# Expert inputs of a two-layer hybrid transformer: rows gathered from DRAM, or made on chip as products with one-hot matrices

## What is computed

```python
def hier_moe(xt, w_rg, b_rg, w_re, b_re, w_g, w_u, w_d):
    lg = xt @ w_rg + b_rg                      # 4 groups
    gi = argmax(lg)                            # top-1 group
    top_v, top_i = top_k(le_of_group, 2)       # 8 experts in it, the best 2
    wts = pg_top * softmax(top_v)
    ...
    xd = zeros(...).at[dest].set(xt[t_s])      # token rows sorted by expert
    hid = silu(xb @ w_g[e]) * (xb @ w_u[e])    # for each expert e, 1024 -> 256
    yd = hid @ w_d[e]                          # 256 -> 1024
    return zeros(n, d).at[t_s].add(yd[dest] * w_s)
```

## Time and profile before

| | before |
|---|---|
| median of 3 runs | 1564.5 us (1563.03 to 1565.46) |
| the profiled execution: its time / span of its instructions | 1567.55 / 1565.7 us |
| PE busy | 1233.9 us, 79% |
| DVE busy | 598.4 us, 38% |
| ACT busy | 445.4 us, 28% |
| POOL busy | 154.1 us, 10% |
| moved by DMA | 388.11 MB, mean 248 GB/s |

### The profile page before, as it was taken

One profiled execution on the slowest core, in us unless ns is written; L12 is line 12 of the kernel. 1 busy time (PEld: TensorE's weight loads), 2 busy tenths in 40 slices (PEclk: granted clock), 3 DMA queues, 4 the chain that ended last, 5 costly groups with the idle time before them and its releaser, 6 DMA issues. The chain is left out here.

```text
span 1565.7 us, 20477 instructions
## 1 busy us (share of the span) xinstructions
PE 1233.9 (79%) x8036; PEld 892.6 (57%) x8036; DVE 598.4 (38%) x1223; ACT 445.4 (28%) x993; POOL 154.1 (10%) x147
## 2 busy tenths in 40 slices
PE   3799798999999648888777259988999478788871
PEld 1589665688879535444343149855999344344430
DVE  0534586354454531111110274575677511111102
ACT  1233266533343310000000244355665210001002
POOL 1601000011112210000000330000012200000002
PEclk9899999999999769899899769989999689889996
DMA  9994168623322138999999905358554179999993
GB/s 321 300 387 140 55 216 298 187 88 101 108 81 82 41 138 339 422 422 422 412 422 390 299 27 135 108 186 263 171 170 167 76 291 423 421 423 411 422 423 129
DMA packets 150543, 388.11 MB, mean 248 GB/s; under 512 B 35232, under 2 KB 96672, under 8 KB 125888
## 3 DMA queue, kind: packets, MB, share of 16 engines
q1 hardware_dynamic: 123424, 315.95, 54.5%
q10 hardware_dynamic: 18784, 41.61, 7.1%
q0 software_dynamic: 8256, 29.46, 4.8%
HBM read 346.09 MB, written 40.89 MB: 247 GB/s over the span
## 5 line engine op out<-in xcount | busy, mean ns | idle before, releaser
L1586 DVE TENSOR_TENSOR w_lo<-ring,w_hi 128x256 fp32r<-128x256 f32 x480 | 222.3, 475 | 268.8 <-ACT w_hi L1281 268.3
L1281 ACT ACTIVATE w_hi<-ring 128x256 fp32r<-128x256 f32 x480 | 197.2, 417 | 290.7 <-PE banks L844 260.3
L1062 PE MATMUL banks<-ring,arena 128*64 128x256 f32 x2048 | 242.8, 394 | 25.7 <-issue 16.7
L844 PE MATMUL banks<-h_hi,w_hi 128*128 128x512 f32 (+1 forms) x640 | 222.4, 348 | 13.1 <-DVE w_lo L1586 10.4
L844 PE MATMUL banks<-h_lo,w_hi 128*128 128x512 f32 (+1 forms) x640 | 220.6, 345 | 0.0
L1076 PE MATMUL banks<-ring,att 128*64 128x512 f32 x512 | 155.4, 763 | 82.7 <-DMA ring<-in_w_e_down 43.6
L844 PE MATMUL banks<-h_hi,w_lo 128*128 128x512 f32 (+1 forms) x640 | 220.4, 344 | 0.0
L1062 PEld LDWEIGHTS banks<-ring,arena 128*64 128x64 f32 x2048 | 154.4, 141 | 104.3 <-issue 29.3
L1076 PEld LDWEIGHTS banks<-ring,att 128*64 128x64 f32 x512 | 47.1, 172 | 175.8 <-issue 125.4
L844 PEld LDWEIGHTS banks<-h_hi,w_hi 128*128 128x128 f32 x640 | 122.8, 192 | 29.9 <-DVE h_lo L1578 7.9
L1407 ACT ACTIVATE arena<-banks 128x1024 f32<-128x1024 f32 x32 | 32.7, 1023 | 349.8 <-PE banks L1076 342.7
(11 more groups left out here) (179 smaller groups left out, 1521.7 us busy)
## 6 DMA issues: line engine op xcount, KB each, us to landing
ring<-in_w_e_gate SPq DMA_DIRECT2D x64, 1024.0 KB, 10.8
ring<-in_w_e_up SPq DMA_DIRECT2D x64, 1024.0 KB, 11.1
ring<-in_w_e_down SPq DMA_DIRECT2D x64, 1024.0 KB, 10.6
ring<-in_w_mod SPq DMA_DIRECT2D x48, 1024.0 KB, 6.0
ring<-in_w_in SPq DMA_DIRECT2D x38, 1024.0 KB, 7.3
arena<-dispatched ACTq DMA_DIRECT2D x32, 512.0 KB, 10.9
expert_rows<-arena ACTq DMA_DIRECT2D x32, 512.0 KB, 7.9
dispatched<-att POOLq DMA_DIRECT2D x24, 512.0 KB, 18.4
```

Source lines behind the costliest of these rows:

```text
L844: ins = mm(out_ap, a, b, start=k == 0 and p_ == 0, stop=k == KD - 1 and p_ == 2)
L1062: ins = mm(banks[e * CAP:(e + 1) * CAP, bank, 0:DE], xeT[b][:, k, e * CAP:(e + 1) * CAP], w[:, k * DE:(k + 1) * DE], start=k == 0, stop=k ...
L1281: fn(w_hi[:, u % AHEAD, :, :], chunk(key)[:, q * KU:(q + 1) * KU, :], ACT.Copy).then_inc(w_hi_ready, 1)
L1586: v.tensor_tensor(w_lo[:, u % AHEAD, :, :], chunk(key)[:, q * KU:(q + 1) * KU, :], w_hi[:, u % AHEAD, :, :].bitcast(F32), ALU.subtract).th ...
```

## The change

The DRAM tensor `xd`, its zeroing (24 of the 32 DMAs of `zero_rows`), the scatter and the reads back are taken out. Instead:

- ACT copies the normalised token rows, rounded to the matmul format, to `th_hi` (over `h_hi`), re-ordered so that channel chunk k stands together; the source is read with a step of 8 elements. POOL subtracts to get the remainder `th_lo` (over `h_lo`), again reading `htok` with that step. These are 4 operations of 128x1024 on each engine in layer 0, and 2 in layer 1. They stand right after the logits' copy to `lgT`.
- For four experts at a time (a "quad", 256 slots) DVE's `select` builds the one-hot matrix `sel` of 128 tokens x 256 slots for each token tile: a comparison into `sel_one` and a second comparison with addition into `sel`, after the slot numbers were lowered by 256. That is 4 + 4 operations of 128x256 per quad in layer 0, 2 + 2 in layer 1.
- PE's `pick_x` multiplies: for each of 8 channel chunks, for each token tile, `th_hi` and `th_lo` (128x128, stationary) with `sel` (256 columns, moving). That is 64 matmuls per quad in layer 0 and 32 in layer 1, in four steps; DVE's `take_xT` copies 128x512 after each step. The 8 transposes per pair go.
- On PE the four steps of the next quad stand in the pair step of the even pair: the first before `step_gu`, the second and third between `step_gu` and `step_d`, the fourth after `step_d`.
- The loop's body is now four pairs, in 2 turns; 8 pairs stand unrolled. `store_y` stays. The constants grow by 256 columns (128 KB). The spill code makes its rows in the same way.

The diff, cut to its core:

```diff
-UNROLL = 4
 NPAIR = NE // 2
-LOOPED = (NPAIR - 6) // 2
+PPI = 4
+LOOPED = (NPAIR - 8) // PPI
+UNROLL = 2 * PPI
+TAIL = NPAIR - 6
+NQUAD = NPAIR // 2
 KU = 1
 AHEAD = 4
...
-        xe = [tile(8, 2), tile(14, 2)]
-        xeT = [tile(2 * b, 2).rearrange("p (k s) -> p k s", k=KD) for b in range(2)]
+        xeT = [tile(4 * b, 4).rearrange("p (k s) -> p k s", k=KD) for b in range(2)]
+        th_hi, th_lo = (h[:, :, :].rearrange("p k n -> p (k n)").rearrange("p (t d) -> p t d", t=4) for h in (h_hi, h_lo))
+        sel = [att_r[:, 1320 + 1024 * b:2344 + 1024 * b].rearrange("p (t s) -> p t s", t=4) for b in range(2)]
+        sel_one = att[:, 3368:4392].rearrange("p (t s) -> p t s", t=4)
+        sel_spill = arena_r[:, 8, 0:4 * CAP].rearrange("p (t s) -> p t s", t=4)
+        sel_spill_one = arena[:, 9, 0:4 * CAP].rearrange("p (t s) -> p t s", t=4)
+        sel_slot = sb("sel_slot", [P, 2, 4])
         act_g = [arena[:, 12 + b, 0:DE] for b in range(2)]
...
-                for dst, first in ((xd, 0), (yd, MAIN)):
-                    for r in range(first // P, ROWS_D // P):
-                        pool.dma_start(dst[r * P:(r + 1) * P, :], zero).then_inc(xd_zero, 16)
+                for r in range(MAIN // P, ROWS_D // P):
+                    pool.dma_start(yd[r * P:(r + 1) * P, :], zero).then_inc(yd_zero, 16)
...
-            def scatter(l):
-                pool.wait_ge(slots_ready, l + 1)
-                if l == 0:
-                    pool.wait_ge(xd_zero, ZEROED)
+            def remainders(l):
                 for tt in range(QT[l]):
-                    for c in range(2):
-                        pool.indirect_dma_start(
-                            out=xd, out_offset=bass.IndirectOffsetOnAxis(ap=slots_u[:, c, tt:tt + 1], axis=0),
-                            in_=htok[:, tt, :], in_offset=None).then_inc(scattered, 16)
+                    pool.wait_ge(th_hi_ready, QT0[l] + tt + 1)
+                    h = htok[:, tt, :].rearrange("p (s k) -> p k s", k=KD)
+                    hi, lo = (x[:, tt, :].rearrange("p (k s) -> p k s", k=KD) for x in (th_hi, th_lo))
+                    pool.tensor_tensor(lo, h, hi.bitcast(F32), ALU.subtract).then_inc(th_lo_ready, 1)
             def combine(l):
...
-            def turn_x(b, n):
-                for k in range(KD):
-                    ins = turn(banks[:, X_BANK + k // 4, k % 4 * P:k % 4 * P + n], xe[b][0:n, k::KD], ident[0:n, 0:n])
+            def pick_x(l, picked, k, out):
+                for tt in range(QT[l]):
+                    for h in (th_hi, th_lo):
+                        ins = mm(out, h[:, tt, k * P:(k + 1) * P], picked[:, tt, :],
+                                 start=tt == 0 and h is th_hi, stop=tt == QT[l] - 1 and h is th_lo)
                 return ins
...
-            def step_x(l, p, i=None):
-                n = E0[l] + p
-                pe.wait_ge(xe_in[n % 2], lin(i, 16 * (n // 2 + 1), 16))
-                if n:
-                    pe.wait_ge(xeT_ready, lin(i, n, 2))
-                hold()
-                turn_x(n % 2, P).then_inc(xe_turned, 1)
+            def step_x(l, d, q, i=None):
+                n = Q0[l] + d
+                if q == 0:
+                    pe.wait_ge(sel_ready, lin(i, n + 1, PPI // 2))
+                if d == 0 and q == 0:
+                    pe.wait_ge(th_lo_ready, QT0[l] + QT[l])
+                if 4 * n + q >= 2:
+                    pe.wait_ge(xeT_ready, lin(i, 4 * n + q - 1, 2 * PPI))
+                for kk in range(2):
+                    ins = pick_x(l, sel[n % 2], 2 * q + kk, banks[:, X_BANK + q % 2, kk * SEQ:(kk + 1) * SEQ])
+                ins.then_inc(xe_turned, 1)
...
+                if p % 2 == 0:
+                    pe.wait_ge(xeT_ready, lin(i, 4 * (n // 2 + 1), 2 * PPI))
+                x = xeT[n // 2 % 2][:, :, p % 2 * P:(p % 2 + 1) * P]
+                widen(x, G_BANK, ws).then_inc(e_gate_done, 1)
...
             def pair_step(l, p, i=None):
+                d = p // 2 + 1
+                ahead = p % 2 == 0 and d < NQUAD
                 step_h(l, p, i)
-                if p + 2 < NPAIR:
-                    step_x(l, p + 2, i)
+                if ahead:
+                    step_x(l, d, 0, i)
                 if p + 1 < NPAIR:
                     step_gu(l, p + 1, i)
+                if ahead:
+                    step_x(l, d, 1, i)
+                    step_x(l, d, 2, i)
                 step_d(l, p, i)
+                if ahead:
+                    step_x(l, d, 3, i)
             def experts(l):
...
+                for tt in range(nt):
+                    fn(th_hi[:, tt, :].rearrange("p (k s) -> p k s", k=KD),
+                       htok[:, tt, :].rearrange("p (s k) -> p k s", k=KD), ACT.Copy).then_inc(th_hi_ready, 1)
...
-            def load_x(l, p, i=None):
-                n = E0[l] + p
-                row = p * P if i is None else act.snap(i * (2 * P) + p * P)
-                act.dma_start(xe[n % 2], xd[bass.ds(row, P), :]).then_inc(xe_in[n % 2], 16)
...
-                if p + 4 < NPAIR:
-                    act.wait_ge(xe_turned, lin(i, n + 3, 2))
-                    load_x(l, p + 4, i)
             def experts(l):
-                act.wait_ge(xd_zero, ZEROED)
-                act.wait_ge(scattered, 32 * (QT0[l] + QT[l]))
-                for p in range(2):
...
+            def equal(l, one, n):
+                for tt in range(QT[l]):
+                    ins = v.tensor_scalar(one[:, tt, :], C["iota_q"][:, 0:n], sel_slot[:, 1, tt:tt + 1], None, ALU.is_equal)
+                return ins
+            def either(l, dst, one, n):
+                for tt in range(QT[l]):
+                    ins = v.scalar_tensor_tensor(dst[:, tt, :], C["iota_q"][:, 0:n], sel_slot[:, 0, tt:tt + 1], one[:, tt, :],
+                                                 ALU.is_equal, ALU.add)
+                return ins
+            def select(l, d, i=None):
+                n = Q0[l] + d
+                slots = sel_slot[:, :, 0:QT[l]]
+                if d == 0:
+                    ins = v.tensor_copy(slots, slots_f[:, :, 0:QT[l]])
+                else:
+                    ins = v.tensor_scalar(slots, slots, -float(SEQ), None, ALU.add)
+                ins.then_inc(sel_slot_ready, 1)
+                dve.wait_ge(sel_slot_ready, lin(i, n + 1, PPI // 2))
+                equal(l, sel_one, SEQ).then_inc(sel_one_ready, 1)
+                if n >= 2:
+                    dve.wait_ge(xe_turned, lin(i, 4 * (n - 1), 2 * PPI))
+                dve.wait_ge(sel_one_ready, lin(i, n + 1, PPI // 2))
+                either(l, sel[n % 2], sel_one, SEQ).then_inc(sel_ready, 1)
...
-            def take_xT(l, p, i=None):
-                n = E0[l] + p
-                if n >= 2:
-                    dve.wait_ge(e_up_done, lin(i, n - 1, 2))
-                dve.wait_ge(xe_turned, lin(i, n + 1, 2))
-                v.tensor_copy(xeT[n % 2], banks[:, X_BANK:X_BANK + 2, :].rearrange("p a (k s) -> p (a k) s", s=P))\
+            def take_xT(l, d, q, i=None):
+                n = Q0[l] + d
+                if q == 0 and n >= 2:
+                    dve.wait_ge(e_up_done, lin(i, 2 * n - 2, PPI))
+                dve.wait_ge(xe_turned, lin(i, 4 * n + q + 1, 2 * PPI))
+                v.tensor_copy(xeT[n % 2][:, 2 * q:2 * q + 2, :], banks[:, X_BANK + q % 2, :].rearrange("p (k s) -> p k s", k=2))\
                     .then_inc(xeT_ready, 1)
             def take_hid(l, p, i=None):
...
             def pair_step(l, p, i=None):
+                d = p // 2 + 1
+                ahead = p % 2 == 0 and d < NQUAD
                 take_hidT(l, p, i)
-                if p + 2 < NPAIR:
-                    take_xT(l, p + 2, i)
+                if ahead:
+                    take_xT(l, d, 0, i)
                 if p + 1 < NPAIR:
                     take_hid(l, p + 1, i)
+                if ahead:
+                    for q in (1, 2, 3):
+                        take_xT(l, d, q, i)
+                    if d + 1 < NQUAD:
+                        select(l, d + 1, i)
             def experts(l):
-                take_xT(l, 0)
-                take_xT(l, 1)
+                select(l, 1)
+                for q in range(4):
+                    take_xT(l, 0, q)
                 take_hid(l, 0)
                 for p in range(2):
                     pair_step(l, p)
                 with dve.Fori(0, LOOPED) as i:
...
```

140 lines of the change are left out of this document (73 added, 67 removed).

## The result

The changed kernel took 1538.8 us (median of 4 runs, 1536.69 to 1541.27), beside 1564.4 us of the kernel before on the same chip: a ratio of 0.9834, interval 0.9819 to 0.9849. A second comparison on another chip gave 1543.3 beside 1566.6 us, 0.9866 (0.9838 to 0.9894). The forecast was 1535.8 us with a range of 1520 to 1549. The profiled execution of after took 1538.04 us, its span is 1536.0 us. It moved 352.75 MB in place of 388.11. Of all executions in this document one, of e8_split, took 4339.7 us for a reason that nothing here shows; it is left out of that kernel's numbers.

The account below looks back on a forecast made before the run. The experts were taken as bound by DMA bytes. Terms +0.3, layer 0 -11.3 and layer 1 -17.7 gave -28.7 us: 1538.9 us from the profiled 1567.55, 1535.8 us against the median, range 1520 to 1549.

Parts of the forecast that it names:

- What bounds it: Experts stage: bound by bytes, 7.34 MB per pair at 422 GB/s, or 17.39 us.
- Rival 5: Experts' stream: slot release sets a round, not bytes, so the change frees nothing; 1564 us, chance 0.04.
- Layer 0's stream: Layer 0's experts: 12 row loads fewer win 14.9 us, less 0.9 for lumped TensorE work: -14.0 us.
- I leave 0.9 us to this: Layer 0's experts: allowance for uneven TensorE work, 19.0 us in even pairs and 11.3 in odd, evened by six slots.
- Rival 3: Layer 0's experts: TensorE sets the pace by a little, with products at 0.15 us; about 1543 us, chance 0.08.
- Layer 1's stream: Layer 1's experts: 12 row loads fewer at 1.24 us each, the stage staying bound by bytes: -14.9 us.
- The fronts: From the slots to SP's first load of the stream: -6.3 us in layer 0, -7.3 in layer 1.
- the prediction's bound: Products on TensorE: starts 0.12 us apart at full clock and 0.24 at half clock.
- The routing: Logits' copy to slots: POOL's subtractions hold DVE's small operations, +9.0 us in layer 0, +4.5 in layer 1.
- Rival 1: Routing: small DVE operations aren't held by POOL, so it is as long as before; 1522.3 us, chance 0.18.
- rival 2: Remainders take 3.31 us each, delays 12 and 6, first products at half clock; 1540.3 to 1547.9 us, chance 0.20.
- What costs nothing: Zeroing, `select` and ACT's four copies of about 1.02 us are free; the constants cost +0.3 us.

Follow-up runs that it names:

- e8_split: Changed kernel with the remainders made by DVE, the first token tile's before its wait for ACT's exponentials, the others behind the slots and first select: 1526.8 us, 0.9765.
- e1_no_row_loads: Kernel before the change, with the row loads of pairs 4 to 15 left out of both layers: 1531.5 us, 0.9789.
- e9_all_ahead: Changed kernel with the last quarter of a quad's products issued ahead of `step_d` in place of behind it: 1552.0 us, 0.9898.
- e6_order: Changed kernel with the third quarter of a quad's products issued behind `step_d` in place of ahead of it: 1536.8 us, 0.9838.
- e3_rem_after_slots: Changed kernel with POOL's subtractions moved behind the slots by one wait for `slots_ready`: 1538.5 us, 0.9847.
- e4_rem_on_dve: Changed kernel with the subtractions done by DVE in place of POOL, ahead of its wait for TensorE's ranks: 1531.2 us, 0.9789.
- e2_pool_beside_routing: Kernel before the change, with only POOL's subtractions added after the logits' copy, their result unused: 1578.2 us, 1.0087.

## Why the prediction was right, point by point

- **What bounds it.** Right, in both layers of the kernel before: e1_no_row_loads gave -14.5 and -16.4 us for 12 loads at 1.24 us. Rival 5 is out.
- **Layer 0's stream: -14.0, measured -8.7.** The step that failed is "I leave 0.9 us to this". TensorE's work per quad was sized well: 31.2 us forecast and 31.1 in the quad shown, and without the products' second half the rounds are bound by bytes; a product cost 0.12 us and the clock was full for most of the stage, as assumed. But the work was costed as if six slots evened out the two rounds of a quad. The price was 6.1 us (276.15 less 270.02), not 0.9: 1.6 to 2.8 of them in the first 55 us and the rest all along the stage. That unevenness costs time is shown by e9_all_ahead, where more of it cost 11.5 us. That it explains all of the 6.1 isn't: e6_order evened the middle rounds and its stream was as long. Rival 3 had the right symptom (an average round of 16.7 us, 394 to 419 GB/s) and the wrong cause: the spacing stayed at 0.12. As the text said, the spacing tells them apart.
- **Layer 1's stream: -14.9, measured -19.0.** -16.4 for the loads, a term that was 1.5 too small, -1.9 at the end, nearly all of it a `step_d` in the last chain that stayed at full clock, and 0.7 unexplained. The rounds are 16.1 us on average where 16.2 were forecast.
- **The fronts: -6.3 and -7.3, measured -9.6 and -7.1.** Layer 1 is right. In layer 0 I had the first quarter of the products at half clock and spread at 6.7 us. In the profile of after the products ran at 0.12 us from the start and spread took 5.14; in the second profile spread took 6.77 and the front 20.6 us. So 1.6 of the 3.3 us is the state of the clock on that occasion and the rest the first quarter, which is at full clock in both. This isn't so in every version: in e8_split some 16 of the first 64 products start 0.21 us apart, which is the spacing at half clock and less than the 0.24 of the prediction's bound. The rows of after:

```profile
575.83 5.14 PE L816 MATMUL banks<-modr,consts 128*128 128x256 f32 x16 [5.54 <-DVE slots_u L1859]
582.09 0.39 PE L1065 MATMUL banks<-att_r,h_hi 128*128 128x256 f32 x1 [1.11 <-ACT gate_t L1250]
582.31 0.28 PE L1065 MATMUL banks<-att_r,h_lo 128*128 128x256 f32 x1
582.43 0.28 PE L1065 MATMUL banks<-att_r,h_hi 128*128 128x256 f32 x1
...
590.83 7.13 PE L1073 MATMUL banks<-ring,arena 128*64 128x256 f32 x64 [0.87 <-DVE arena L1882]
```

- **The routing: +9.0 and +4.5, measured +10.3 and +5.3.** The mechanism is as forecast. POOL's operation was mis-sized: 2.82 us where the nearest row had 2.35, the rest is the step of 8 elements (2.31 without it). The Trainium skill (GPSIMD Engine Reference, Performance pitfalls for Q7 kernels) gives about 50% for such reads; this case's operation, which reads one of its two inputs with the step, shows 22%. The rule of the Trainium skill (SBUF — State Buffer, Who interferes with whom) that a whole instruction excludes the other engine now has rows of this case for small operations. They aren't only those with two on-chip inputs: a cast and a tensor-scalar of 0.17 us ended after 2.76 us as well, while `MAX8` and `FIND_INDEX8` were not held. Rival 1 is out by these rows, and rival 2 came true by about half of its way in POOL's time and the delays, and not with its first products at half clock in layer 0.
- **What costs nothing.** ACT's copies were mis-sized by a factor, 1.97 us each for 1.02. They stayed free where nothing else used the gap: in e3_rem_after_slots, with the same copies and POOL at rest, the slots come after 18.2 us as before. But there DVE waits 3.29 us for the exponentials and then 0.99 for the ranks, in place of 0.27 and 4.02: the copies use up the gap, which e4_rem_on_dve paid for. Zeroing, `select` and the constants show in no stage beyond its spread.
- **The total** was right by luck: in the ledger errors of +5.3, -4.1, -3.3, +1.3 and +0.8 us, the -1.9 of the first stage (-1.6 for +0.3) and the +1.0 between the layers nearly cancel. The median came out 3.0 us over the forecast. A range of 29 us held it easily; what the prediction got right and wrong is read from the ledger, not from the sum.

## What to carry to other kernels

When an engine's work is moved onto one that is nearly full, fit it round by round against the transfer's time per round, not as a mean over several; where TensorE's work stood within 5% of the transfer's time, the products cost 6.1 us of the 14.5 that leaving out the loads gives in the same layer, some at the start and the rest all along the stage. A helper engine that works beside a chain of tiny operations on DVE can hold each of them for the length of its own instruction: place such work in the chain's real gaps, measured in the changed kernel and not in the one before, and look at what the next DVE work is before moving it later. Put the re-ordering of data into the copy that is made once (1 us more on ACT), not into the operand that TensorE loads 768 times.

## What the runs showed of the hardware

- A weight load of 128x128 in the rounded format with a step of 8 elements took 0.34 us against 0.19, and the matmuls behind such loads started 0.24 us apart against 0.12. With contiguous matrices and a granted clock of 0.50 (layer 1 of e8_split) they started 0.21 us apart.
- A copy of 128x1024 on ACT took 0.97 us in natural order and 1.97 with a source step of 8 elements; the subtraction with one such input 2.31 and 2.82 us on POOL, 1.93 on DVE.
- While POOL ran one subtraction of two on-chip tensors, a `TENSOR_TENSOR`, a `CAST` and a `TENSOR_SCALAR` of 0.17 us each on DVE took 2.65 to 2.77 us; four `MAX8` beside it (in e2_pool_beside_routing) kept their 0.37 us together.
- 16 matmuls of 512 columns took 3.65 us at a granted clock of 1.00 and 5.35 us at a mean of 0.68. The idle time just before them didn't decide it alone: in after they took 5.35 us behind 2.02 us and 3.65 us behind 2.66.
